# A recurrent layer turned token-major: 512-column unit pairs in a two-block transformer kernel

## The reference, cut to what matters

```python
def even_layer(x, g_pre, g_post, w_in, b_gate, conv_w, conv_b, gn_g, gn_b, hn_g, w_out):
    h = rms_norm_2(x, g_pre)
    a_val, a_gate, z_a, q, k, v, o, z_b, gates = split_cols(h @ w_in, EVEN_SIZES)
    u = depthwise_conv_centred(a_val * sigmoid(a_gate), conv_w, conv_b)
    y_a = silu(group_layer_norm(u, gn_g, gn_b, A_GROUPS)) * silu(z_a)
    ...
    h_fwd = mlstm_chunkwise(qh, kh, vh, i_f, f_f)
    h_bwd = fl(mlstm_chunkwise(fl(qh), fl(kh), fl(vh), fl(i_b), fl(f_b)))
    hm = (h_fwd + h_bwd).transpose(0, 2, 1, 3)          # tokens x 4 heads x 256
    hm = rms_norm_2(hm, hn_g.reshape(H_B, DV_B))        # mean of squares over a head's 256
    hm = sigmoid(o) * hm
    y_b = hm.reshape(B, S, W_B) * silu(z_b)
    y = concatenate([y_a, y_b], axis=-1) @ w_out
    return x + rms_norm_2(y, g_post)
```

## Time and profile before

| | |
|---|---|
| median of 3 runs | 836.91 us (836.58 to 837.25) |
| profiled execution | 837.42 us, of which the span of its instructions is 835.6 us |
| TensorE busy | 827.6 us (99%) |
| VectorE / ScalarE / GpSimd busy | 567.3 / 495.8 / 24.5 us |
| chain that ended last | TensorE 96% |
| mean granted TensorE clock | 0.998 of 2.4 GHz |

### The profile page before, as it was taken

One profiled execution on the slowest core, in us unless ns is written; L12 is line 12 of the kernel. 1 busy time (PEld: TensorE's weight loads), 2 busy tenths in 40 slices (PEclk: granted clock), 3 DMA queues, 4 the chain that ended last, 5 costly groups with the idle time before them and its releaser, 6 DMA issues.

```text
span 835.6 us, 14089 instructions
## 1 busy us (share of the span) xinstructions
PE 827.6 (99%) x5442; PEld 733.0 (88%) x5442; DVE 567.3 (68%) x1050; ACT 495.8 (59%) x847; POOL 24.5 (3%) x30
## 2 busy tenths in 40 slices
PE   9999999999999999999999999999999999999997
PEld 7998898889878888888878799999998889999785
DVE  6443446867967777785876766467886575669765
ACT  5655457765476666565574345766675574665454
POOL 0000000003400000000000000000000001000000
PEclk9999999999999999999999999999999999999999
DMA  9755752226535555556535444443445644545212
GB/s 333 295 212 217 271 184 102 102 102 208 180 127 200 202 190 170 195 170 230 184 114 210 152 148 154 151 142 120 145 173 200 227 152 165 188 151 202 102 51 75
DMA packets 21837, 144.08 MB, mean 172 GB/s; under 512 B 2545, under 2 KB 3185, under 8 KB 5136
## 3 DMA queue, kind: packets, MB, share of 16 engines
q1 hardware_dynamic: 20880, 140.50, 47.0%
q10 hardware_dynamic: 896, 2.73, 1.0%
HBM read 142.17 MB, written 1.05 MB: 171 GB/s over the span
## 4 chain that ended last, share of the span: by engine, by line
PE 96%; DVE 1%; ACT 1%; DMA 1%; SPq 0%; issue 0%; DVEq 0%; ACTq 0%
PE PS L479 94%; DMA ring<-w 1%; PE PS L960 0%; PE PS L1382 0%; ACT PB L1512 0%; PE PS L733 0%; PE PS L961 0%; PE PS L962 0%; ACT wh L1472 0%; DVE xb L2442 0%; DVE xa L2439 0%; PE PS L1205 0%; DVE PB L2631 0%; PE PS L1246 0%; ACT hx L1486 0%
## 5 line engine op out<-in xcount | busy, mean ns | idle before, releaser
L2076 DVE TENSOR_TENSOR wl<-ring,wh 128x1024 fp32r<-128x1024 f32 x248 | 305.8, 1237 | 194.7 <-ACT wh L1472 192.5
L479 PE MATMUL PS<-hx,wh 128*128 128x256 f32 (+1 forms) x2088 | 398.8, 303 | 0.4 <-DVE hx L2145 0.3
L1472 ACT ACTIVATE wh<-ring 128x1024 fp32r<-128x1024 f32 x247 | 260.5, 1057 | 213.1 <-PE PS L479 192.0
L479 PEld LDWEIGHTS PS<-hx,wh 128*128 128x128 f32 x2088 | 329.1, 191 | 16.6 <-issue 4.5
L479 PE MATMUL PS<-hx,wl 128*128 128x256 f32 x1212 | 282.9, 283 | 0.0
L479 PE MATMUL PS<-wh,hx 128*128 128x512 f32 (+2 forms) x832 | 223.3, 376 | 0.0
L479 PEld LDWEIGHTS PS<-hx,wl 128*128 128x128 f32 x1212 | 208.6, 191 | 3.4
L479 PEld LDWEIGHTS PS<-wh,hx 128*128 128x128 f32 x832 | 150.8, 188 | 28.6 <-issue 2.1
L479 PE MATMUL PS<-wl,hx 128*128 128x512 f32 (+2 forms) x416 | 131.1, 372 | 0.1
L479 PEld LDWEIGHTS PS<-wl,hx 128*128 128x128 f32 x416 | 77.7, 188 | 14.4 <-DVE wl L2076 1.1
L1763 ACT ACTIVATE T<-PS 128x512 f32<-128x512 f32 x22 | 13.2, 598 | 27.0 <-PE PS L479 27.0
(11 more groups left out here) (303 smaller groups left out, 664.7 us busy)
## 6 DMA issues: line engine op xcount, KB each, us to landing
ring<-w SPq DMA_DIRECT2D x127, 1024.0 KB, 4.8
cn<-consts SPq DMA_DIRECT2D x2, 1051.0 KB, 11.4
V<-gains ACTq DMA_DIRECT2D x3, 512.0 KB, 6.1
cn<-consts SPq DMA_DIRECT2D x1, 1050.5 KB, 10.5
xa<-x SPq DMA_DIRECT2D x2, 512.0 KB, 4.5
out<-xb SPq DMA_DIRECT2D x4, 256.0 KB, 2.1
ring<-w SPq DMA_DIRECT2D x2, 256.0 KB, 4.9
ring<-w SPq DMA_DIRECT2D x1, 512.0 KB, 7.6
```

What stands on the lines that cost most here:

```text
L479: return nc.tensor.matmul(o, lhsT, rhs, start=start, stop=stop, skip_group_check=True)
L1472: A(wh[:, q % SPLITS, :], ring[:, i % RING, e:e + HALF], ACT.Copy).then_inc(sem("hi_ready"), 1)
L2076: TTn(wl[:, q % SPLITS, :], ring[:, PLACE[unit_of(q)] % RING, e:e + HALF], wh[:, q % SPLITS, :].bitcast(F32), ALU.subtract).then_inc(sem(" ...
```

## The change

The layer's v, o and z are computed with tokens on partitions. Instead of twelve units of 256 columns there are six *pairs* of units of 512 columns (`EVEN_PAIRS`: v, o, z of heads 0 and 1, then v, z, o of heads 2 and 3), each four halves of 12 matmuls with 512 moving weight columns (`pair_half`), in two PSUM banks. Pairs alternate between banks 0, 1 and banks 5, 7; all 24 halves are in the table. A head's output is now tokens x 256: `pv` has the weights' transpose stationary and the values moving. ScalarE squares it and sums along the free axis in the same instruction (`accum_out`), so the GpSimd add and the averaging product go, and Ln and Exp work on two columns. `yb` is one multiply-multiply per token tile; its result is token-major and is transposed on TensorE (`lstm_back`, `back`, eight 128 x 128 transposes for two heads) into PSUM, from which the split for the output projection is read, with the head gain as its scale. Four halves of the output projection, not three, go into each `deep` part.

```diff
+EVEN_PAIRS = (("v", 0), ("o", 0), ("z", 0), ("v", 1), ("z", 1), ("o", 1))
...
-EVEN_STEPS = []
-for _h in range(4):
-    EVEN_STEPS += [[("weigh", _h)] if _h else [("decay", 0)], [("yb", _h - 1)] if _h else [("weigh", 0)], [],
...
-EVEN_HALVES = 22
-EVEN_EARLY = 3
+EVEN_STEPS = [
...
+    [("gn_x", 3), ("gn_y", 1), ("gn_t", 2)], [("gn_y", 2), ("gn_t", 3)], [("turn", 1), ("zg", 0), ("oz", 0)],
+    [("yb", 0), ("gn_y", 3)], [("pv", 1)], [("decay", 2)], [("weigh", 2), ("yb", 1)], [], [("turn", 2)],
...
+EVEN_HALVES = 24
+EVEN_EARLY = 4
...
+        def lstm_out(h):
+            return PS[:, AV[0] if h < 3 else PAIR_SETS[0][1], :]
...
-            wide_a(v_unit(0))
+            def pair_half(i, n):
+                if n == 0 and i >= 2:
+                    pe.wait_ge(*pair_read(i - 2, 1))
+                if n == 0 and i == 0:
+                    for u in (2, 3):
+                        pe.wait_ge(*read(FIRST["z_a"] + u))
...
+                def term(h_, w_, start=False):
+                    for kk in (2 * n, 2 * n + 1):
+                        for t in range(TT):
+                            m = mm(pair_bank(i, t), h_[:, kk, t * P:(t + 1) * P], w_[:, kk % 2 * 512:(kk % 2 + 1) * 512],
+                                   start and kk == 0, False)
+                    return m
+                a = high_half_in(q)
+                term(hh, a, True)
+                term(hl, a)
+                _, b = half_in(q)
+                half_out(term(hh, b))
...
             def lstm_pv(h):
                 pe.wait_ge(sem("lstm_wT"), h + 1)
-                pe.wait_ge(*read(v_unit(h)))
-                if h >= 1:
+                pe.wait_ge(*pair_read(3 * (h // 2), 1))
+                if h == 3:
+                    pe.wait_ge(*pair_read(4, 1))
+                elif h:
                     pe.wait_ge(sem("yb_done"), h)
...
-            def lstm_var(h):
-                pe.wait_ge(sem("squares_summed"), h + 1)
-                mm(PS[:, AV[1], 0:S], c("mean", P, 2 * P), T1[:, 0, 0:S], True, True).then_inc(sem("lstm_var"), 1)
...
+            def lstm_back(p):
+                pe.wait_ge(sem("yb_done"), 2 * p + 2)
+                for h in (2 * p, 2 * p + 1):
+                    for e in range(2):
+                        for t in range(TT):
+                            m = nc.tensor.transpose(y_turned(8 + 2 * h + e)[:, t * P:(t + 1) * P],
+                                                    y_rows(h, t)[:, e * P:(e + 1) * P], ident)
+                    m.then_inc(sem("lstm_turned"), 1)
...
                     if kind == "deep":
                         if n == 0:
                             pe.wait_ge(sem("lstm_decay_read"), 16)
                             pe.wait_ge(sem("lstm_scores_read"), 16)
+                            pe.wait_ge(*pair_read(5, 1))
...
             for i, step_ in enumerate(EVEN_STEPS):
                 if i < EVEN_HALVES:
+                    multiplied(half_of("v_o_z") + i)
+                    if i % 4 == 3:
+                        even_evac(i // 4)
...
                     elif kind == "pv":
                         act.wait_ge(sem("lstm_h"), n + 1)
-                        A(T1[:, 0, :], PS[:, AV[0], :], ACT.Square).then_inc(sem("squares"), 1)
-                    elif kind == "var":
-                        act.wait_ge(sem("lstm_var"), n + 1)
-                        A(RSH, PS[:, AV[1], 0:S], ACT.Ln, bias=eps_t[:, 0:1]).then_inc(sem("lstm_rs"), 1)
+                        ms = hss[:, 2 * n:2 * n + 2]
+                        for t in range(TT):
+                            A(RSH[:, t * S:(t + 1) * S], lstm_out(n)[:, t * S:(t + 1) * S], ACT.Square, scale=0.25,
+                              accum_out=ms[:, t:t + 1]).then_inc(sem("squares"), 1)
+                        act.wait_ge(sem("squares"), 2 * n + 2)
+                        A(ms, ms, ACT.Ln, bias=eps_t[:, 2:3]).then_inc(sem("lstm_rs"), 1)
                         act.wait_ge(sem("lstm_rs"), 2 * n + 1)
-                        A(RSH, RSH, ACT.Exp, scale=-0.5).then_inc(sem("lstm_rs"), 1)
+                        A(ms, ms, ACT.Exp, scale=-0.5).then_inc(sem("lstm_rs"), 1)
...
             for k in range(8, 16):
-                if k in (8, 14):
-                    act.wait_ge(sem("yb_done"), 3 if k == 8 else 4)
-                deep_high("even_out", Y, EVEN_OUT, k)
+                act.wait_ge(sem("lstm_turned"), LH + (k - 8) // 2 + 1)
+                act.wait_ge(sem("half_used"), half_of("even_out") + k - 7)
+                high(k % 8, y_turned(k), "deep_hi", scale=v("hn_g", k - 8))
                 halves(half_of("even_out") + k + 1)
```

More of the change, by code:

```diff
@@ L182 @@
 GATE_HALVES = [min(s, len(GATE_PARTS)) for s in range(NP + PV_LAG + 1)]
-EVEN_STEPS = []
-for _h in range(4):
-    EVEN_STEPS += [[("weigh", _h)] if _h else [("decay", 0)], [("yb", _h - 1)] if _h else [("weigh", 0)], [],
[L190 to L197, removed]
-EVEN_HALVES = 22
-EVEN_EARLY = 3
+EVEN_STEPS = [
+    [], [("spread", 0)], [("decay", 0)], [("weigh", 0)], [("gn_x", 0)], [("gn_x", 1), ("gn_t", 0)], [("turn", 0)],
+    [("pv", 0), ("gn_y", 0), ("gn_t", 1)], [("decay", 1), ("gn_x", 2)], [("weigh", 1)],
+    [("gn_x", 3), ("gn_y", 1), ("gn_t", 2)], [("gn_y", 2), ("gn_t", 3)], [("turn", 1), ("zg", 0), ("oz", 0)],
+    [("yb", 0), ("gn_y", 3)], [("pv", 1)], [("decay", 2)], [("weigh", 2), ("yb", 1)], [], [("turn", 2)],
+    [("pv", 2), ("decay", 3)], [("weigh", 3), ("zg", 1)], [], [("turn", 3), ("split", 0)], [("pv", 3), ("split", 1)],
+    [("deep", 0), ("oz", 1)], [("yb", 2), ("yb", 3), ("back", 0)], [("deep", 1)], [("back", 1)]]
+EVEN_HALVES = 24
+EVEN_EARLY = 4
 UQ_HALF = [half_of("w_uq") + n if n < 6 else half_of("w_uk") + (n - 6) // 2 if n < 10 else
@@ L1814, in gate_logs, with even_evac @@
                 A(lfx, lfx, ACT.Ln, bias=1.0).then_inc(sem("lstm_exp"), 1)
-            units = v_unit(0) + 1 - FIRST["conv_in"]
+            def even_evac(i):
+                kind, p = EVEN_PAIRS[i]
+                if kind == "z" and p:
+                    act.wait_ge(sem("oz_ready"), p)
+                for t in range(TT):
+                    if kind == "v":
+                        A(V[:, t, p * 512:(p + 1) * 512], pair_bank(i, t), ACT.Copy).then_inc(pair_read(i, t)[0], 1)
+                    elif kind == "o":
+                        A(gate_rows(p, t), pair_bank(i, t), ACT.Tanh, scale=0.5).then_inc(pair_read(i, t)[0], 1)
+                    else:
+                        A(T1[:, t, :], pair_bank(i, t), ACT.Tanh, scale=0.5).then_inc(sem("z_tanh"), 1)
+            units = FIRST["v_o_z"] - FIRST["conv_in"]
             for n in range(units):
@@ L1833, in _ @@
                         A(RS4, PS[:, 4, :], ACT.Ln, bias=eps_t[:, 1:2]).then_inc(sem("gn_rs"), 1)
-                    if half == 0 and n == 16:
-                        act.wait_ge(sem("gn_rs"), 1)
-                        A(RS4, RS4, ACT.Exp, scale=-0.5).then_inc(sem("gn_rs"), 1)
                     if half:
@@ L2181, in _ @@
             dve.wait_ge(sem("nsa_tanh"), 1)
-            TS(gnsa, gnsa, 1.0, 0.5, ALU.add, ALU.mult).then_inc(sem("nsa_gates"), 1)
+            own(TS(gnsa, gnsa, 1.0, 0.5, ALU.add, ALU.mult))
             def values_in(p, t, n):
@@ L2508, in _ @@
             weigh_spectrum(0, 2)
-            for i in range(18):
+            for i in range(16):
                 halves(half_of("qk") + i + 1 + SPLITS)
@@ L2534, in _ @@
             for s_, step_ in enumerate(EVEN_STEPS):
-                if s_ < EVEN_HALVES and s_ != 18:
-                    halves(half_at(o_unit(0)) + s_ + 1 + SPLITS)
+                if s_ < EVEN_HALVES:
+                    halves(half_of("v_o_z") + s_ + 1 + SPLITS)
                 for kind, n in step_:
@@ L2814, in _ @@
                     .then_inc(sem("merged"), 1)
-            for h in range(LH):
-                pool.wait_ge(sem("squares"), h + 1)
-                nc.gpsimd.tensor_tensor(T1[:, 0, 0:S], T1[:, 0, 0:S], T1[:, 0, S:2 * S], ALU.add)\
-                    .then_inc(sem("squares_summed"), 1)
-            pool.wait_ge(sem("squares"), LH + 1)
+            pool.wait_ge(sem("squares"), 2 * LH + 1)
             for a, b in ((0, 1), (3, 4), (0, 2)):
                 if b == 2:
-                    pool.wait_ge(sem("squares_summed"), LH + 1)
+                    pool.wait_ge(sem("squares_summed"), 1)
                 nc.gpsimd.tensor_tensor(LS[:, a, :], LS[:, a, :], LS[:, b, :], ALU.add)\
```

120 lines of the change are left out of this document (60 added, 60 removed).

## The result

The changed kernel takes 847.66 us (median of 4 runs, 846.76 to 848.63) against 836.80 (median of 4, 836.58 to 837.25): a ratio of 1.0129 [1.0117, 1.0141], 1.3% slower. The forecast was 847.0 in 841 to 852.5. Its profiled execution took 846.76, the fastest of the four, the span 844.9. I measure the recurrent layer from TensorE's gate sums (or, before, the v unit ahead of them) to the first transposes behind the output projection: 669.57 - 537.22 = 132.35 us before, 678.82 - 536.25 = 142.57 now, +10.2.

A forecast was written before the change was run, and what follows sets the result against it. TensorE's own work was taken to set the end (busy 827.6 of 835.6 us). Work -4.0, waits +12.5 and clock +1.7 gave +10.2 on 837.4: 847.6, so 847 us for the median, range 841 to 852.5.

The forecast's parts named there:

- halves of 512 columns: TensorE's 24 halves: 2.72 us each with 512-column products for 2.88 with 256, 3.9 us less work.
- `var` gone: TensorE's four averaging products dropped, at 0.5 us each: 2.0 us less work.
- `back`: TensorE's 16 new transposes of the head outputs, in two groups of eight: 1.9 us more work.
- work together: TensorE's net change in work over the layer: -4.0 us.
- first half: Layer's start: the first pair takes both banks, so TensorE waits for the last z_a activation, 1.4 us.
- second `pv`: Second head's product waits for the first head's `yb`, behind 20.1 us of VectorE's queue: 5.5 us (4.5 to 6.3).
- third, fourth turn: TensorE waits at these heads' `turn` for the chain from the preceding `pv` through `weigh`: 1.5 and 2.2 us.
- output projection, behind `back`: Waits for ScalarE to free pair 5's banks, 0.8 us, and for the first half behind the second `back`, 1.1.
- clock: Granted clock falls in the long wait, so the second `pv` and halves behind it run slow: 1.7 us, bounds 0 to 3.
- the rival of a second fall: Clock stays down behind `pv`, or the fourth turn's wait brings another fall: +15, 852 us; chance 0.15.
- queues keep up: ScalarE splits half 11 in time and only the bank wait at the start costs: -2.6, 834.3 us; chance 0.06.
- The waits without a fall of the clock: All forecast waits in the layer come but the clock stays up: 845.4 us; chance 0.17.

The follow-up runs named there:

- e9: Against e8: each 512-column product of the pairs written as two of 256 columns; 837.52 us, ratio 1.0008.
- e10: Against e8: one unread fp32 product put back at each of the four places where `var` stood; 835.72 us, ratio 0.9987.
- e8: Changed kernel with rewritten order table, last z_a activation and evacuations (steps 11, 23) ahead of ScalarE's splits, and later eleventh output-projection split; 833.93 us, ratio 0.9967.
- e2: Changed kernel with twelve fp32 products into an unread bank issued on TensorE in the wait ahead of the second `pv`; 845.96 us, ratio 1.0111.
- e1: Changed kernel, table only: convolution-branch parts (`gn_x` 2, 3, `gn_y` 1 to 3, `gn_t` 1 to 3) moved behind the first `yb`; 848.25 us, ratio 1.0142.
- e7: Changed kernel, table only: same parts in another order, branch spread over steps where VectorE stood idle, second `pv` one step later; 838.68 us, ratio 1.0018.
- e6: Changed kernel with the split of the output projection's eleventh half put behind turned outputs 8 and 9 on ScalarE and VectorE; 847.14 us, ratio 1.0125.
- e4: Changed kernel with each 512-column product of the six pairs written as two of 256 columns; 849.35 us, ratio 1.0151.
- e5: Changed kernel with ScalarE taking the last z_a activation and the sixth pair's evacuation (step 23) ahead of the splits; 845.36 us, ratio 1.0101.
- e3: Changed kernel with `Ln` and `Exp` of the head's mean square replaced by copies, so no table loads there; 844.99 us, ratio 1.0090.

## Why the prediction was right, step by step

| step | forecast | measured |
|---|---|---|
| halves of 512 columns | -3.9 | -3.3 to -3.6 (e9) |
| `var` gone | -2.0 | -1.8 (e10) |
| `back` | +1.9 | +1.6 to 1.8 (0.79 a group from start to start, and up to 0.1 in the products behind it) |
| work together | -4.0 | -2.8 in the changed kernel, -3.3 in e8 |
| first half | 1.4 | 1.37 |
| second `pv` | 5.5 | 5.41 |
| third, fourth turn | 1.5, 2.2 | 1.08, 1.51 |
| output projection, behind `back` | 0.8, 1.1 | 0.98, 0.94 and, for the low part, 0.4 |
| clock | 1.7 | 1.6 to 1.7 (e2) |
| sum | +10.2 | -2.8 + 11.3 + 1.7 = +10.2 |

The sum closes by construction: the -2.8 is what is left of the layer's +10.2 when the six gaps and the clock are taken off.

**The mechanism** held at each place. The count of VectorE's queue was the step that carried the forecast: 20.1 us forecast, 20.4 found, and e1 and e7 show by moving parts of it that it is what the second `pv` waits for. The chain from the first `pv` came out at 26.7 for 26.5, TensorE's side at 21.3 for 21.0.

**The sum fits better than its terms.** By the table work was 1.2 us dearer than forecast and the waits 1.2 shorter. Of that 0.4 is only a matter of where it is booked: the wait for the low part behind the second `back`, which my 1.1 included, is no gap between groups of products, so it fell into the rest called work; e6 and e8 are without it. The other 0.8 is two errors that cancelled. Work: a half behind another kind of product costs more than the 2.72 I gave each, as from 570.52 to 573.48 behind scores, 2.96; by e9 the halves are 0.3 to 0.6 of it, and by e10 the `var` terms, whose 0.5 each was not what their removal gives, 0.2. `back` was 0.1 to 0.3 cheaper than forecast, so up to 0.6 is not found. Waits: in part the same thing, for the slower TensorE is, the less it waits. For the third turn TensorE's side was 12.7 (from 596.18 to 608.90) for 12.4 forecast while the chain was 13.8 for 13.9. In the fourth it was more the chain: 11.4 for 11.9, the squares taking 0.86, not 1.2. That the rest of the two errors is of one size is luck. The profiled execution is 0.8 us under my 847.6: the layer began 1.0 us earlier in it (536.25 for 537.22).

**The clock** cost what I said, for reasons that were half right. I forecast it to fall 2.6 us into the wait and to stay low for 5.9 us of work, of which slack at the third turn would give a part back. It fell 5.4 us in, as work came back, stayed low for 3.4 us, which is `pv` and little more, and gave nothing back. What I had described is what e4 and e5 show, with 6.8 us of low clock and a shorter third turn. I had given the rival of a second fall 0.15; in the changed kernel's profiled execution there was none, in e1, e3 and e7 there was one in a place that I had not named. Of the changed kernel's four runs the profiled one is the fastest; the two slowest (847.84 and 848.63) have a mean clock of 0.994 for its 0.996, which points to more low clock in them, and the median stands 0.7 above my 847.0. No trace shows where.

**Two rules weighed.** Two products of 256 columns in place of one of 512 cost 3.6 us over the layer where nothing waits (e9). By the gap of 2.5 ns per matmul that the Trainium skill states for the isolated case (TensorE: Matmul & The Clock Gate, Back-to-back issue gap), without a weight load for each matmul, it would be 0.7, an estimate for 288 products more; the measurement decides. Two loads of 1.28 us stand in each pair of Ln and Exp, as before, and e3, without them, took 2.3 us of waits from the two turns. The Trainium skill (ScalarE: Activation LUTs, Table sets: the hidden batching unit) has Ln and Exp in one set; this program did not load them so.

**Rivals.** The faster one (queues keep up, 834.3) failed at the place it named: `yb` stands one half before the `pv` that needs it. With the table of e7 and the other order changes its mechanism is what happens, at 833.9. The waits without a fall of the clock (845.4) are what e2 built, at 846.0; in the kernel as changed the clock fell, and all four runs have a mean clock of 0.994 to 0.996.

## What to carry to other kernels

Where one engine has no idle time, count what stands in another's queue between two hand-overs, in its order, and compare that with the first engine's work in between; busy shares say nothing of it (VectorE's is 67% with 11 us of waits and 68% without). Before a layer is judged, try its order: the same instructions took 847.7 and 838.7 us, and 833.9 with three more exchanges of neighbours. Measure a gain in work where nothing waits: the wider products were worth 3.6 us there and 1.7 in the kernel as changed.
